# A three-term split matmul: passes over all k-steps in place of three matmuls per k-step

## What is computed

```python
for l in range(DEPTH):                       # DEPTH = 2
    hn = rmsnorm(x, norm_mix_pre[l])
    if l % 2 == 0:                           # mixer_even: gated MLP || RG-LRU
        z = hn @ w_in                        # 1024 -> 2048: u, v, xb, gb
        u = gelu(u); v = rmsnorm(gelu(v))
        a_out = u * (masked w_s @ v + b_s)   # in chunks of 128 frames, 4 heads
        xc = causal_dwconv(xb) + conv_b
        r, i = sigmoid(xc @ wa + ba), sigmoid(xc @ wx + bx)
        h = scan(exp(-8 r softplus(-lam)), ...)   # h[t] = a[t] h[t-1] + b[t]
        m = concat(a_out, h * gelu(gb)) @ w_out
    else:                                    # mixer_odd: gated short convolution
        bg, cg, xv = split(hn @ w_in, 3)     # 1024 -> 3072
        m = (bg * causal_dwconv(cg * xv)) @ w_out
    x = x + rmsnorm(m, norm_mix_post[l])
    hn = rmsnorm(x, norm_ffn_pre[l])
    f = square(relu(hn @ mlp_up[l])) @ mlp_down[l]     # 1024 -> 4096 -> 1024
    x = x + rmsnorm(f, norm_ffn_post[l])
```

## Time and profile before

| | us |
|---|---|
| median of 3 runs | 2289.5 (2289.11 to 2290.53) |
| profiled execution | 2288.14 |
| its span, first to last instruction | 2286.3 |
| PE busy in it | 2206.0 (96%) |
| DVE / ACT / POOL busy | 894.6 / 678.7 / 154.7 |
| mean granted TensorE clock | 0.985 |

### The profile page before, as it was taken

The page is one execution under the profiler, slowest core; times in us unless marked ns, Lnnn a source line. Parts: engine busy times, 40 slices in busy tenths (PEclk is TensorE's granted clock), DMA queues, the critical chain, the costliest instruction groups (busy, mean ns, idle before and its releaser), DMA issues.

```text
span 2286.3 us, 32182 instructions
## 1 busy us (share of the span) xinstructions
PE 2206.0 (96%) x13817; PEld 2189.8 (96%) x13817; DVE 894.6 (39%) x1320; ACT 678.7 (30%) x1160; POOL 154.7 (7%) x143
## 2 busy tenths in 40 slices
PE   7986899999999999999899999999999999999997
PEld 7976899999999999999899999999999999999997
DVE  3636426632332232233674333275223323322335
ACT  5554334420220230133431111354103202202333
POOL 0113400000000000000014223000000000000000
PEclk9998999999999999999999999999999999999999
DMA  6110133111111111113221111331111111111132
GB/s 206 49 29 20 38 132 97 54 47 47 47 47 47 47 47 47 47 47 132 63 79 47 47 47 55 113 97 57 46 46 47 47 46 47 47 47 47 47 132 77
DMA packets 228737, 143.02 MB, mean 63 GB/s; under 512 B 5084, under 2 KB 227252, under 8 KB 228596
## 3 DMA queue, kind: packets, MB, share of 16 engines
q1 hardware_dynamic: 228304, 140.89, 20.3%
q10 hardware_dynamic: 292, 0.08, 0.0%
HBM read 119.22 MB, written 21.73 MB: 62 GB/s over the span
## 4 chain that ended last, share of the span: by engine, by line
PE 92%; DVE 4%; ACT 2%; issue 2%; DMA 0%; ACTq 0%; DVEq 0%
PE ps L684 30%; PE ps L685 30%; PE ps L686 30%; DVE v_tok L1548 1%; PE ps L765 1%; PE ps L722 1%; DVE f L1364 0%; PE ps L738 0%; PE ps L790 0%; DVE w_all L1330 0%; DVE f L1348 0%; DVE lru L1515 0%; PE ps L731 0%; ACT v_junk L1170 0%; DMA vec_rows<-in_norm_ffn_post_dram 0%
## 5 line engine op out<-in xcount | busy, mean ns | idle before, releaser
L684 PE MATMUL ps<-x_hi,w_all 128*128 128x352 f32 x2328 | 763.9, 328 | 8.9 <-DVE xb_pad L1444 5.4
L685 PE MATMUL ps<-x_lo,w_all 128*128 128x352 f32 x2328 | 750.2, 322 | 0.0
L686 PE MATMUL ps<-x_hi,w_all 128*128 128x352 f32 x2328 | 749.7, 322 | 0.0
L684 PE MATMUL ps<-h_hi,w_all 128*128 128x352 f32 x1728 | 561.7, 325 | 0.8 <-DVE h_lo L1567 0.8
L686 PE MATMUL ps<-h_hi,w_all 128*128 128x352 f32 x1728 | 556.3, 322 | 0.0
L685 PE MATMUL ps<-h_lo,w_all 128*128 128x352 f32 x1728 | 556.1, 322 | 0.0
L684 PEld LDWEIGHTS ps<-x_hi,w_all 128*128 128x128 f32 x2328 | 440.2, 189 | 12.3 <-issue 6.3
L685 PEld LDWEIGHTS ps<-x_lo,w_all 128*128 128x128 f32 x2328 | 440.9, 189 | 2.3 <-issue 0.3
L686 PEld LDWEIGHTS ps<-x_hi,w_all 128*128 128x128 f32 x2328 | 439.6, 189 | 0.0
L916 ACT CAST w_all<-w_all_raw 128x1024 fp32r<-128x1024 f32 x169 | 176.9, 1046 | 514.6 <-DMA w_all_raw<-in_mlp_down_dram 319.5
L684 PEld LDWEIGHTS ps<-h_hi,w_all 128*128 128x128 f32 x1728 | 326.2, 189 | 1.1 <-DVE h_lo L1567 1.0
(11 more groups left out here) (190 smaller groups left out, 1546.2 us busy)
## 6 DMA issues: line engine op xcount, KB each, us to landing
w_all_raw<-in_mlp_up_dram SPq DMA_DIRECT2D x60, 512.0 KB, 4.0
w_all_raw<-in_mlp_down_dram SPq DMA_DIRECT2D x60, 512.0 KB, 4.1
x_save<-f SPq DMA_DIRECT2D x12, 1408.0 KB, 6.4
x_old<-x_save SPq DMA_DIRECT2D x12, 1408.0 KB, 11.5
w_all_raw<-in_c_w_in_dram SPq DMA_DIRECT2D x22, 512.0 KB, 3.8
w_all_raw<-in_w_in_even_dram SPq DMA_DIRECT2D x15, 512.0 KB, 3.9
x_rows<-in_x_prompt_dram SPq DMA_DIRECT2D x8, 512.0 KB, 6.7
w_all_raw<-in_w_out_even_dram SPq DMA_DIRECT2D x6, 512.0 KB, 4.2
```

The lines of the kernel that those rows point to most:

```text
L684: nc.tensor.matmul(dst, wh, hi, start=(i == 0), stop=False)
L685: nc.tensor.matmul(dst, wh, lo, start=False, stop=False)
L686: last = nc.tensor.matmul(dst, wl, hi, start=False, stop=(i == KC - 1))
```

## The change

Inside a unit there are now three loops over the k-steps in place of one: first all eight high x high matmuls, then all eight with the low activations, then all eight with the low weights. The waits before a k-step (`x_ready`, `h_part`) all stand in the first loop. `between(n, i)` is called in the first loop for i = 0 to 3 and in the second for i = 4 to 7. Instructions, their number and their operands are the same, and so is what is added up; only the order within a unit differs. Nothing is changed on other engines.

```diff
                 phase = START.index(max(s for s in START if s <= n))
+                dst = bank(n)
                 for i, k in enumerate(order):
                     if X and n - START[phase] in (0, 4, 8):
                         pe.wait_ge(x_ready, 24 * phase + 8 * t + k + 1)
                     if u.m == 0:
                         h_part(n, i)
-                    hi, lo = pt(src[0], k, t), pt(src[1], k, t)
-                    wh, wl = w_k(l, 0, k), w_k(l, 1, k)
-                    dst = bank(n)
-                    nc.tensor.matmul(dst, wh, hi, start=(i == 0), stop=False)
-                    nc.tensor.matmul(dst, wh, lo, start=False, stop=False)
-                    last = nc.tensor.matmul(dst, wl, hi, start=False, stop=(i == KC - 1))
-                    if i == KC - 1:
-                        last.then_inc(pe_unit, 1)
-                    between(n, i)
+                    nc.tensor.matmul(dst, w_k(l, 0, k), pt(src[0], k, t), start=(i == 0), stop=False)
+                    if i < KC // 2:
+                        between(n, i)
+                for i, k in enumerate(order):
+                    nc.tensor.matmul(dst, w_k(l, 0, k), pt(src[1], k, t), start=False, stop=False)
+                    if i >= KC // 2:
+                        between(n, i)
+                for i, k in enumerate(order):
+                    last = nc.tensor.matmul(dst, w_k(l, 1, k), pt(src[0], k, t), start=False, stop=(i == KC - 1))
+                last.then_inc(pe_unit, 1)
```

## The result

The changed kernel takes 2340.9 us (median of 4 runs, 2338.3 to 2342.8) where the kernel before took 2289.3 beside it: the ratio is 1.0225, 95% interval 1.0207 to 1.0243. The forecast was 2307.5, at most 2320. The sign was right, and the size was wrong by 33 us: +51.6 came where +18 was forecast.

A forecast was written before the change was run, and what follows sets the result against it. PE, busy 96% of the span, was taken as the bound. Operand waits +1.27, gates and transposes +6.6, spatial +3.5, start -0.3, turns +5.4 make +16.5; with clock +1.5, 2306.1 profiled, 2307.5 median; range 2288 to 2320.

The forecast's parts named there:

- The distance between matmuls: In the large matmul stream on PE, the spacing stays at 0.159 us, so the new order itself costs nothing.
- Rival B: In the large matmuls, sweeping high and low operands lengthens the distance to that of slot x: +27 us, 2334; chance 0.12.
- Rival D: In PE's operand reads, the distance shrinks by over 1.8 ns a matmul; at 4 ns, 53 us less, 2254; chance 0.06.
- The recorded durations: L684 is recorded 6 ns longer than L685; if weight reload caused it, 13.7 to 26 us would go.
- Moved waits: Operand waits and small work placed earlier in units make PE stand longer: +16.5 us at full clock.
- rival E: Moved waits in phase 0 and at turns are partly swallowed as releases move too: 2297.7; chance 0.12.
- the fixed release: At PE waits set by an earlier unit's end, release stays; matmuls the wait is moved past run after it, 0.159 us each.
- step (a): At the first down units, the MLP's `h_ready` wait after 7 matmuls stays free, with 3.8 us left.
- Clock: Behind unit 19's longer wait, one added half-clock stretch costs +1.5 us.
- the other reading: Lengthened waits at the turns could each bring a half-clock stretch, 1.6 us each: some +5 in place of +1.5.
- Unit 48: First unit of the even projection back: 8 matmuls now run after the release, +1.27 us, lasting 6.1 instead of 4.9.

The follow-up runs named there:

- x2_weights_apart: Kernel before with the last two matmuls of each k-step swapped, so matmuls sharing the high weights never stand adjacent; 2290.4 us in one run.
- s1: Old matmul order of the kernel before, with only the operand waits and small work at the changed kernel's places; 2310.1 us, ratio 1.0095.
- p1: New order with small work at old places; in units 90 to 235 odd k-steps read 128 bytes off, so start parity stays constant; window 558.7 us.
- x8: Kernel before, still k-step by k-step, but even k-steps first, so start parity changes once in a unit; 2294.4 us in one run.
- p2: Kernel before, with some moving-operand reads in units 90 to 235 shifted 128 bytes so start parity alternates at every matmul; 2299.6 us.
- s2: New matmul order of the changed kernel, with small work at the matmul counts of the kernel before; 2321.9 us, ratio 1.0141.

## Why the forecast was wrong, by its steps

**The distance between matmuls: the step that failed.** The forecast took 0.159 us and gave as the reason that this mean was the same for all 146 units, "whose operands lie at all the places that the new order uses". That holds for the places, but not for their succession. Every place had been read in a row of three with its like, and no stretch of before, the window included, had one that changes at each matmul. The price: 2.7 ns a matmul in the long stretches, 29 us in all. Rival B had said that the distance would grow because "operand places matter" and came near the size (2 ns, 27 us, 2334), yet it got 0.12, since I set the agreement of the 146 units against it. The unit of slot x was the one row in which the distance depended on something, and such an exception tells more than a mean that is constant over cases which all share one pattern. But that B came so near in size is luck: in slot x it is the weights that lie elsewhere, and these very units didn't pay the full price. The unit of the earlier trace rows is unit 57, block 0; units 58 and 59 are blocks 1 and 2 with the same weights. First units 58 and 59 before, then units 57 to 59 changed:

```profile
327.29:331.13 3.84, 3.84 (x26) 1.00 0.01 1
331.13:335.00 3.87, 3.87 (x27) 1.00 0.00 0
```

```profile
340.68:344.50 3.82, 3.82 (x25) 1.00 0.47 137
344.50:348.36 3.86, 3.86 (x26) 1.00 0.00 0
348.36:352.18 3.82, 3.82 (x26) 1.00 0.00 0
```

Blocks 0 and 2 got 0.04 us faster, and block 1 only 0.02 slower. In slot x the weights of k-step k start 33k + 22 times 128 bytes into the tile of x, so that their parity changes with k as well, and is that of the moving operand in blocks 0 and 2; in the rotating slots it never changes. So the 161.7 ns hold for weights of constant parity, and the place of the weights counts too. No run varied it by itself.

The forecast did say that it fails if the distance moves by 1 ns. Rival D (a shorter distance) has nothing for it but such units of slot x and the 17 units named below; its threshold, 18 + 4.6 us over 13248, comes to 1.7 ns, not 1.8.

**The recorded durations** said nothing on the distance. L684 was recorded 6 ns longer than L685, but x2_weights_apart, which parts them, has the same window. In the changed kernel the three lines are recorded with 329, 327 and 324 ns while the distance grew by 2.7:

```profile
L682 PE MATMUL ps<-x_hi,w_all 128*128 128x352 f32 x2328 | 439.8, 329 | 7.9 <-DVE xb_pad L1446 4.4
L686 PE MATMUL ps<-x_lo,w_all 128*128 128x352 f32 x2328 | 434.3, 327 | 0.0
L690 PE MATMUL ps<-x_hi,w_all 128*128 128x352 f32 x2328 | 424.2, 324 | 0.0
```

**Moved waits: right in kind and nearly in size.** Alone they cost 20.8 us (interval 18.1 to 25.2 by the ratio), for 18 forecast; so they weren't swallowed (rival E). The gates of units 12 and 19 in the changed trace (start, us, line; in brackets the wait):

```profile
81.11 0.86 PE L767 MATMUL ps<-lru,gate_w 128*128 128x353 f32 x2 [1.64 <-ACT lru L1136]
...
117.64 1.55 PE L767 MATMUL ps<-lru,gate_w 128*128 128x353 f32 x2 [3.41 <-ACT ig L1136]
...
123.42 0.66 PE L778 MATMUL ps<-ident,gelu 128*128 128x128 f32 x4 [1.12 <-ACT v_tok L1162]
```

Unit 12's gate stood 0.37 and now 1.64, +1.27, to the digit; the unit lasts 7.56 in place of 6.24. Unit 19's stood 2.64 and now 3.41; the unit lasts 2.56 longer (2.70 in s1), for 1.27 and a half-clock stretch of 1.5 forecast. Unit 13 gave +0.6 and 20 +0.5 (0.46 each forecast). Unit 26 gave -0.5, since half-clock matmuls went from it and from unit 25, which doesn't last longer at all (+0.64 forecast). What the forecast lacked were half-clock stretches in units 27 (+2.4 for 0.8) and 33 (+2.8 for 1.3). Unit 33 had one before as well, but in front of its wait, where the fixed release hid it; now it stands behind the wait. At the turns the column sums wait 2.9, 7.3 and 2.9 (3.1, 7.5 and 3.4 forecast; by the forecast's own +0.95 on 2.2 the last should read 3.1); the spreads have +1.9 in three waits, 0.63 each (0.64 forecast). No matmul waits for `h_lo` of the MLP, so step (a) holds.

**Clock.** Windows of the changed kernel in units 19, 27, 33 and 359, at 1.2 GHz:

```profile
119.30:120.90 1.60, 1.60 (x7) 0.50 0.00 0
170.20:171.50 1.30, 1.30 (x6) 0.50 0.00 0
225.30:226.80 1.50, 1.50 (x7) 0.50 0.00 0
...
1563.60:1567.90 4.30, 4.30 (x16) 0.50 1.02 306
```

By the start times, distances between the large matmuls near 0.293 us (those of half clock) number 113 before, 125 in s1 and 142 in the changed kernel: at 0.134 us each, +1.6 us for s1 and +3.9 for the full change, for +1.5 forecast. Right in the sum for s1, but not in place: units 25 and 26 lost the half clock, 19 and 27 have it now, and in 33 it moved behind the wait. At the turns 56 such distances became 67 in s1 and 70 in the changed kernel, +1.5 and +1.9 us, and not the +5 that the forecast gave as the other reading. The trace agrees in kind with the Trainium skill, "TensorE: Matmul & The Clock Gate", section "Why this matters for your kernels" (idle gaps between bursts of matmuls bring the slow clock back): the waits of 3.4 us in units 19 and 359 and of 2.4 us in unit 27 were followed by these stretches.

**Unit 48** is the cleanest check of both. s1 gives 6.10 us, the forecast's 6.1 for 4.9. Its wait, s1 first and the changed kernel behind it:

```profile
303.35 0.43 PE L685 MATMUL ps<-h_lo,w_all 128*128 128x352 f32 x1 [2.01 <-DVE h_lo L1567]
```

```profile
304.77 1.05 PE L682 MATMUL ps<-h_hi,w_all 128*128 128x352 f32 x4 [2.00 <-DVE h_lo L1569]
305.62 2.55 PE L686 MATMUL ps<-h_lo,w_all 128*128 128x352 f32 x8
```

The wait is the same 2.0 (0.76 before), but behind it s1 runs at full clock and the changed kernel at half: 8 matmuls in a good 2.3 us, and the unit lasts 7.68. The windows behind the wait, s1 and then changed:

```profile
303.70:306.60 2.90, 2.90 (x20) 1.00 1.13 367
```

```profile
305.70:308.60 2.90, 2.90 (x12) 0.50 1.09 369
```

A wait of the same length may bring the half clock or not; the waits of 2.0 us in unit 48 are of that kind. What decides between them isn't shown.

**The sum.** 29.2 for the distance, the moved waits' 21.0 and 2.3 for the half clock that the changed kernel has beyond s1 (3.9 less 1.6, most of it in unit 48) make 52.5, against 52.2 in the spans. To take the window's 2.7 ns for all 13248 matmuls would give 35 us for the distance, which is too much: outside the long stretches the mean went only from 159.9 to 161.0 ns, by 1.2.

Left open: what in the chip makes the parity of 128 bytes matter, whether steps smaller than 128 bytes matter too, and why a few units escape. Units 252 to 254 of the changed kernel have their weights in the rotating slots and alternate like all others, but repeat 156 161 156 160 and take 3.800 each, less than any unit of before (there they take 3.840). 17 units in all take 3.80; twelve of them are the three behind a unit of slot x at each of the four turns. So the same addresses were read at two different distances; what else decides, and how the kernel gets into the fast pattern, wasn't tried.

## What to carry to other kernels

Before the order of a long matmul stream is changed, write down the start addresses in the order in which they will be read, and look whether the trace holds a stretch with that succession; a mean over other successions says nothing, and 2.7 ns in 159 made more than half of the loss here. Small work and waits inside such a stream count by the number of matmuls ahead of them: where another engine's release is fixed, each matmul that the wait is moved past is lost, and moving it later wins it back until a later chain takes over. Test the two halves of such a change apart; each has its own row in the trace.

## What the runs showed of the hardware

TensorE's distance between matmuls of 352 fp32r columns, each with its own weight load from a place of constant parity, depends on where the moving operand starts in SBUF, here compared in steps of 128 bytes: 160.0 ns with all starts on one parity, 158.3 with all on the other, 159.0 with three and three, and 161.7 when it alternates at every matmul (p1, x8, the kernel before, p2). Shifting one read in three by 128 bytes is enough to move a stretch from 557.07 to 566.48 us. Neither the order in which the weights were read, 512 bytes apart, nor loading the same weights twice in a row changed it. With weights whose start also changes parity at each matmul (slot x) it was 159.3 ns in blocks 0 and 2 and 160.8 in block 1, where before it had been 161.0 and 160.0. And the same addresses gave 161.7 ns in most units and 158.3 in units 252 to 254.

The same wait of 2.0 us in unit 48 was followed by half clock in the changed kernel (and in s2, 7.68 us too) and not in s1 (6.10 us).
